# Two edits to the order of work in a two-block transformer kernel: when weight blocks are prepared in the odd output projection, and the order of VectorE's work ahead of its attention

## The reference

```python
z = h @ w_in                                   # cq, ckv, kr, xr, xg
q = (rmsnorm(cq, g_cq) @ w_uq)                 # qn, qr = rope(...)
kv = (rmsnorm(ckv, g_ckv) @ w_ukv)             # kn, v
yc = dense_mla(qn, qr, kn, rope(kr), v)        # 8 heads, softmax over all 512 keys
yd = rglru_block(xr, xg, ...)                  # conv, sigmoid gates, scans in both directions, times gelu(xg)
x = x + concatenate([yc, yd]) @ w_out
x = x + sq_relu_mlp(rmsnorm(x, norm_mlp[1]), w_mlp1[1], w_mlp2[1])
```

## Time and profile before

| | |
|---|---|
| time, median of 3 (lowest, highest) | 1582.22 us (1581.96, 1589.49) |
| the profiled execution: time, span | 1582.22 us, 1580.4 us |
| mean granted clock of TensorE | 0.974 of 2.4 GHz |
| PE, DVE, ACT, POOL busy | 1477.2, 777.6, 613.2, 566.9 us |
| weight blocks on POOL (L619) | 232 of 2446 ns in the mean |
| weight load, issue to landing | 3.4 us in the median |

### The profile page before, as it was taken

How to read it: one execution, slowest core, us unless ns; L and a number is a source line. 1 busy time by engine, 2 the same in 40 slices (tenths; PEclk the granted TensorE clock), 3 DMA queues, 4 the chain that set the end, 5 groups by cost and what they waited for, 6 DMA issues and landing times.

```text
span 1580.4 us, 20392 instructions
## 1 busy us (share of the span) xinstructions
PE 1477.2 (93%) x7122; PEld 1153.1 (73%) x7122; DVE 777.6 (49%) x1405; ACT 613.2 (39%) x1110; POOL 566.9 (36%) x236
## 2 busy tenths in 40 slices
PE   6989899999999999889899999999988799899997
PEld 5656678888888887446678888888866677666785
DVE  6774442223444678884442223444655236565434
ACT  5443422233222437654332233223443244564431
POOL 3312244444444344111244444444323442122341
PEclk9999999999999999899999999999989999999998
DMA  5211233223222232100122223223213222111221
GB/s 210 76 54 54 67 102 97 93 94 106 93 93 98 76 107 80 41 27 29 66 93 93 93 93 107 93 94 105 81 55 106 93 94 78 43 54 42 74 72 54
DMA packets 36624, 129.55 MB, mean 82 GB/s; under 512 B 4048, under 2 KB 4176, under 8 KB 36560
## 3 DMA queue, kind: packets, MB, share of 16 engines
q1 hardware_dynamic: 35136, 124.80, 24.0%
q10 hardware_dynamic: 1424, 3.90, 0.7%
HBM read 126.58 MB, written 2.10 MB: 81 GB/s over the span
## 4 chain that ended last, share of the span: by engine, by line
issue 57%; POOL 22%; PE 17%; DVE 2%; ACT 1%; POOLq 1%; DVEq 0%; ACTq 0%
POOL w L619 22%; PE bank L636 4%; PE bank L638 4%; PE bank L637 4%; PE bank L761 1%; PE bank L775 1%; PE bank L741 1%; DVE arena L2150 0%; POOLq L618 0%; POOLq L616 0%; ACT tmp L1241 0%; DVE arena L1776 0%; DVE arena L2040 0%; ACT tmp L1231 0%; ACT arena L1522 0%
## 5 line engine op out<-in xcount | busy, mean ns | idle before, releaser
L619 POOL TENSOR_TENSOR w<-raw,w 128x1024 fp32r<-128x1024 f32 x232 | 566.6, 2446 | 979.6 <-ACT w L1183 600.0
L636 PE MATMUL bank<-opC,w 128*128 128x512 f32 x624 | 256.8, 412 | 28.7 <-POOL w L619 14.2
L638 PE MATMUL bank<-opC,w 128*128 128x512 f32 x624 | 247.4, 396 | 0.0
L637 PE MATMUL bank<-opC,w 128*128 128x512 f32 x624 | 247.0, 396 | 0.0
L1752 DVE TENSOR_TENSOR mlp_op<-arena,mlp_op 128x512 fp32r<-128x512 f32 x64 | 144.5, 2260 | 188.7 <-ACT mlp_op L1298 188.7
L1270 ACT ACTIVATE w<-raw 128x1024 fp32r<-128x1024 f32 x126 | 133.2, 1057 | 239.5 <-PE bank L638 239.5
L636 PE MATMUL bank<-mlp_op,w 128*128 128x512 f32 x544 | 212.2, 390 | 3.1 <-ACT arena L1388 1.4
L638 PE MATMUL bank<-mlp_op,w 128*128 128x512 f32 x544 | 211.7, 389 | 0.0
L637 PE MATMUL bank<-mlp_op,w 128*128 128x512 f32 x544 | 211.7, 389 | 0.0
L636 PE MATMUL bank<-opA,w 128*128 128x512 f32 x416 | 163.0, 392 | 4.1 <-DVE x L1670 1.8
L636 PEld LDWEIGHTS bank<-opC,w 128*128 128x128 f32 x624 | 120.0, 192 | 59.6 <-issue 14.5
(11 more groups left out here) (215 smaller groups left out, 1931.9 us busy)
## 6 DMA issues: line engine op xcount, KB each, us to landing
raw<-stream_dram SPq DMA_DIRECT2D x232, 512.0 KB, 3.4
out_t_dram<-arena SPq DMA_DIRECT2D x8, 256.0 KB, 2.2
x<-x_t_dram SPq DMA_DIRECT2D x4, 256.0 KB, 5.7
x<-x_t_dram ACTq DMA_DIRECT2D x4, 256.0 KB, 6.9
rope<-ropes_dram ACTq DMA_DIRECT2D x2, 512.0 KB, 6.8
con<-consts_dram ACTq DMA_DIRECT2D x1, 993.5 KB, 8.1
arena<-p_t_dram ACTq DMA_DIRECT2D x1, 512.0 KB, 4.4
par<-params_dram ACTq DMA_DIRECT2D x1, 253.5 KB, 3.8
```

What stands on the lines that cost most here:

```text
L619: pool.tensor_tensor(w_lo[:, j, :], raw[:, j, :], w_hi[:, j, :].bitcast(F32), ALU.subtract).then_inc(lo_made, 1)
L636: pe.matmul(out, wh, hi, start=first, stop=False)
L637: pe.matmul(out, wh, lo, start=False, stop=False)
L638: return pe.matmul(out, wl, hi, start=False, stop=last)
```

## The change

In ACT's program, `oout_row` prepares one block less ahead of each row. In DVE's program, `lru_scan(1)` moves ahead of the eviction of `oin_b` 2, `lru_sum(0)` ahead of those of `mq` 0 and 1, and rotation 6 ahead of `lru_scan(3)` and of the sum behind it.

```diff
             def oout_row(m):
-                prepare(SUB0["oout_b"] // SUBS + 4 + m // 4)
+                prepare(SUB0["oout_b"] // SUBS + 3 + m // 4)
                 act.wait_ge(z_ready, TILE0["oout_b"] + m + 1)
...
             lru_scan(0)
+            lru_scan(1)
             scaled("oin_b", 2, z1(OIN[11]))
+            lru_sum(0)
             scaled("mq", 0, mla["qr"][0], 1)
             scaled("mq", 1, mla["qn"][0], 1)
-            lru_scan(1)
-            lru_sum(0)
             lru_scan(2)
+            rotate(6, mla["qr"][0], P, 3, (tmp[:, 2, :], tmp[:, 3, :]))
             lru_scan(3)
             TTn(decay_tmp(1), decay_tmp(1), states(5), ALU.add).then_inc(part_scanned, 1)
             dve.wait_ge(part_scanned, 1)
-            rotate(6, mla["qr"][0], P, 3, (tmp[:, 2, :], tmp[:, 3, :]))
```

## The result

| | before | after |
|---|---|---|
| time, median of 6 (lowest, highest) | 1587.74 us (1581.96, 1589.73) | 1598.92 us (1596.27, 1600.74) |
| the profiled execution: time, span | 1582.22, 1580.4 us | 1600.61, 1598.8 us |
| mean granted clock in it | 0.974 | 0.964 |

The ratio is 1.0078 (95% interval 1.0054 to 1.0100), which is +12.4 us (8.6 to 15.9), and in a second set of runs 1.0069 (1.0056 to 1.0082), which is +11.0 us (8.9 to 13.0). The kernel is slower, as forecast, and both intervals hold the +9.5 us of the forecast. The time itself, 1598.92, lies 7.2 us above the 1591.7 of the forecast and 3.4 us above the range that ended at 1595.5. Two executions of the kernel before, of 2930 and 4885 us, are slow ones and are left out everywhere.

The account below looks back on a forecast made before the run. PE, busy 93% of the span, was taken to bound the kernel. The terms 8.6 + 0.9 = +9.5 us on 1582.2 gave 1591.7 us; likeliest 1589.5 to 1593.5, with rivals 1586.3 to 1595.5.

Parts of the forecast that it names:

- Part A: `oout_row` and head of `up1`: row 0 gains 1.23 us, but PE waits for the late third block; +8.6 us (+7.8 to +9.5).
- the slow clock behind the head: Head of `up1`: after PE's gap of about 9.3 us, its 66 matmuls lose 2.3 us at half clock.
- the wait's 6.26: Head of `up1`: third tile starts at 793.03 instead of 786.77, +6.26 us, with the 1.23 gained already in it.
- Part B: DVE's order ahead of the attention: who waits for whom changes; +0.9 us, between -0.8 and +3.9.
- steps 1 to 4: Ahead of the attention: eviction +4.71 us, delays passed on, mostly absorbed by the 5.58 us gap; first scores +0.6, second +0.7.
- the slow clock ahead of the attention: `lru_b` tiles 4 to 7 and `mv`, after a 6.0 us PE gap: 0.2 us, with 3.2 us as bound.
- The third block ready anyway: Head of `up1`: B+5 complete before 785.5, so PE would not stall; 1581.9 us, 4 in 100.
- The attention earlier and at full clock: Attention: L1680 escapes POOL, PE starts at 641.3 at full clock; -4.0 instead of +0.9, 1586.8 us, 15 in 100.
- The late eviction comes through at 1.2 GHz: `lru_b` and `mv`: PE's 6 us gap leaves them at half clock; +3.9 instead of +0.9, 1594.7 us, 17 in 100.

Follow-up runs that it names:

- number 6: The changed kernel once more, unaltered, in more rounds: 1599.12 us, ratio 1.0069 against the kernel before.
- Number 1: The kernel before with the edit of `oout_row` alone: 1592.93 us, ratio 1.0044.
- number 8: The kernel before with `oout_row` preparing B+3 ahead of row 0 and both B+4 and B+5 ahead of row 4: 1585.26 us, ratio 0.9988.
- Number 5: The kernel before once more, unaltered, for a second profile: 1587.36 us.
- 2: The kernel before with the changed DVE order alone, `oout_row` as before: 1588.66 us, ratio 1.0009.
- number 3: The kernel before with `lru_scan(1)` and `lru_sum(0)` ahead of the evictions, rotation 6 left at its old place: 1579.07 us, ratio 0.9954.
- number 4: The kernel before with rotation 6 ahead of `lru_scan(3)`, evictions at their old place: 1581.71 us, ratio 0.9970.
- 9: The kernel before with scan and sum ahead of the evictions, rotation 6 unmoved, and B+4 and B+5 prepared ahead of row 4: 1579.98 us, ratio 0.9969.
- 10: The kernel before with rotation 6 ahead of `lru_scan(3)`, evictions unmoved, and B+4 and B+5 prepared ahead of row 4: 1586.14 us, ratio 0.9991.
- number 13: The kernel before with 20 unread matmuls in PE's 5.6 us gap ahead of the attention: 1582.67 us, ratio 0.9967.
- 15: The kernel before with the changed DVE order alone, plus unread matmuls ahead of `lru_b` (24) and the second scores (12): 1586.39 us, ratio 0.9992.
- number 7: The changed kernel with unread matmuls in three PE gaps: ahead of `lru_b`, the second scores and the head's third tile: 1590.07 us, ratio 1.0025.
- 11: The changed kernel with unread matmuls ahead of `lru_b` and of the second scores only: 1594.34 us, ratio 1.0047.

## Why the prediction was right in its steps and wrong in its time

**Part A, the mechanism: right.** B+5 is made behind row 7, PE waits 9.27 us (9.3 forecast) and everything behind waits along. Row 0's low part took 0.75 us as forecast. From row 0 to the third tile the changed kernel took 29.66 us and before 22.60: 7.06 instead of 6.26. The other 0.8 lies between rows 3 and 4, which are 7.96 us apart instead of 7.16; the clock is at 0.50 there in both kernels. In the execution of number 6 they are 6.89 apart, so this is the clock's variation and not the edit. Behind the wait the slow clock took 2.6 (2.3 forecast). Number 1 gives +7.0 for the edit in the mean, number 8 that the cause is the block.

**The term that was off in part A.** I set the slow clock behind the head, 2.3 us, against a head that runs at 1.00 in the kernel before. Number 5 shows the same head at 0.50 in an execution of before, 18.0 us to the sums (787.81 to 805.79). The ten profiles in which the third block was in time (before, numbers 2 to 5, 8 to 10, 13, 15) have 15.1 us five times, 16.7 twice and 18.0 three times, 16.3 in the mean; the four with the late block and no filling have 17.5. So the slow clock behind the wait costs about 1.2 us more than before, not 2.3. With the wait's 6.26 this makes +7.5, and the +8.6 measured +7.0.

**Part B, steps 1 to 4: right in kind, near in size.** From a common start 0.4 us later, the eviction came 4.7 us late (4.71), the gap of 5.58 shrank to 1.12 (1 to 1.5), L1680 was caught by POOL and took 2.41 us, and the second scores wait for L1703. They start 1.6 - 0.4 = 1.2 us late instead of 0.7: `lru_b` ran at 0.50 until 636.5, the rotation's matmul ended at 639.76, 0.9 later than the forecast's 638.46 with the common 0.4, and DVE waited 5.13 us for it. The 0.2 for the slow clock ahead of the attention was too small. In number 7, where this stretch ran at 1.00, both scores come 0.5 us later than before, counted from the end of `lru_scan(0)`, near the 0.6 and 0.7 of the forecast without its clock term. Alone the edit measured +1.4 (forecast +0.9).

**What the steps did not hold.** They ended at the second scores. PE waits there for 3.0 us, and behind the wait the clock was at 0.50 (650.46, scores in 4.09 us instead of 2.19); with the wait filled, in number 7, it stayed at 1.00. The prediction names the wait but gives no price for the clock behind it. Numbers 7 and 11 show that filling gaps is worth 7.0 and 3.5 us in the changed kernel, number 13 that it is worth 5.2 us in the kernel before. So, as far as the intervals tell, the slow clock costs both kernels about as much, and little of it is left in their difference.

**The step that failed: the base of the sum.** I wrote "The profiled execution took 1582.22 us (span 1580.4), which is also the median" and added 9.5 to it. That execution belongs to the fastest fifth of the kernel before; two of the three times in the table were of that kind by luck, and the 1589.49 beside them was no outlier but a time of the slowest group, which has 28 of the 100. From the median of 1587.3 of the 100 executions the same sum gives 1596.8, which is inside the runs of the changed kernel (1596.3 to 1600.7). So the base makes 5.1 of the 7.2 us by which the forecast missed. The other 2.1 are the difference between the +9.5 of the terms and the change as measured, and cannot be told from nothing, since its intervals hold 9.5. My range took in the bounds of the change's terms and none for the state of the clock in the base, which alone spans 8 us.

**The rivals.** The third block ready anyway: refuted by the 9.3 us wait. The attention earlier and at full clock: its condition, that L1680 escapes POOL's operation, held in none of the runs with the rotation or the scan moved (2.41 us in the changed kernel and in number 3, 2.64 in number 4, instead of 0.69). Half of it came true: the first scores ran at full clock, 2.19 us instead of 4.08, but at 643.65 and not at 641.3, and the reductions behind the scan took the gain back. Number 3 keeps the gain of the clock, number 4 brings the earlier start. The late eviction comes through at 1.2 GHz: the clock was low until 636.5, yet it was not this that cost; number 3 has the same gap and is the fastest kernel of all.

**What stays open.** How the 7 us of number 7 divide between attention and head, whether the halves (+8.4) and the whole (+11.0) really differ, where number 3 gains more than the 2.7 us at its second scores, and what decides which group an execution of one kernel falls into.

## What to carry to other kernels

Find the consumer that is the first to need the last of a set of prefetched blocks, and put off a prefetch only as far as that; here one block too late made a wait of 1.8 us into one of 9.3, for 1.2 gained. Where an engine must wait for another in any case, put work of its own into the wait and not behind it: two moves that each gained 5 to 7 us lost their gain together, since the one made the other wait. And before adding a change to a base, look whether the profiled execution is a typical one. Three times are too few for that where the times come in groups; the group is then part of the forecast.

## What was not expected of the hardware

The kernel's time has four groups, 1582 to 1590 us, each with a granted clock of its own (0.975 to 0.965); in the two executions that were profiled, of different groups, PE's gaps are the same; behind the same gap of 1.78 us PE ran at 1.00 in one execution and at 0.50 in another. Matmuls whose results nobody reads, put into gaps of PE, made the kernel before 5.2 us and the changed kernel 7.0 us faster. Put where the clock has fallen already, 32 of them took 10.42 us instead of 7.56 and overran the gap.
